# Turning the gated networks' products in 32x32 blocks on VectorE and through memory, in place of TensorE transposes

## The reference, cut to what matters

```python
def _swiglu(xn, w_gate, w_up, w_down):
    return (jax.nn.silu(xn @ w_gate) * (xn @ w_up)) @ w_down

f = _swiglu(_rmsnorm(h, ffn1_pre_g[i]), ffn1_w_gate[i], ffn1_w_up[i], ffn1_w_down[i])
h = h + 0.5 * _rmsnorm(f, ffn1_post_g[i])
# the token mixer stands between the two
f = _swiglu(_rmsnorm(h, ffn2_pre_g[i]), ffn2_w_gate[i], ffn2_w_up[i], ffn2_w_down[i])
h = h + 0.5 * _rmsnorm(f, ffn2_post_g[i])
```

## Time and profile before

| | us |
|---|---|
| median of 3 runs | 1149.78 (1149.68 to 1149.98) |
| the profiled execution's own time | 1149.85 |
| its span, first to last instruction | 1148.1 |
| TensorE busy in it | 1137.0 |
| VectorE busy | 741.5 |
| ScalarE busy | 589.3 |
| GpSimd busy | 106.0 |

### The profile page before, as it was taken

One profiled execution on the slowest core, in us unless ns is written; L12 is line 12 of the kernel. 1 busy time (PEld: TensorE's weight loads), 2 busy tenths in 40 slices (PEclk: granted clock), 3 DMA queues, 4 the chain that ended last, 5 costly groups with the idle time before them and its releaser, 6 DMA issues.

```text
span 1148.1 us, 16462 instructions
## 1 busy us (share of the span) xinstructions
PE 1137.0 (99%) x6408; PEld 993.1 (86%) x6408; DVE 741.5 (65%) x931; ACT 589.3 (51%) x788; POOL 106.0 (9%) x162
## 2 busy tenths in 40 slices
PE   9999999999999999999999999999999999999997
PEld 8998888888889999988888898899888888889885
DVE  6866686657777888754664554665866566545465
ACT  6774654445565766543544443564554364444353
POOL 6410211000011000000000000200500010000020
PEclk9999999999999999999999999999999999999999
DMA  9743653465634765564665556465457477654642
GB/s 258 206 156 92 223 187 111 161 202 185 218 130 141 251 205 175 188 213 148 213 211 182 187 177 207 152 217 179 146 186 238 147 229 235 191 169 175 218 132 72
DMA packets 122894, 209.81 MB, mean 183 GB/s; under 512 B 10965, under 2 KB 58186, under 8 KB 122827
## 3 DMA queue, kind: packets, MB, share of 16 engines
q1 hardware_dynamic: 119225, 198.64, 54.2%
q10 hardware_dynamic: 3506, 10.23, 2.7%
q0 software_dynamic: 96, 0.01, 0.1%
HBM read 207.67 MB, written 1.18 MB: 182 GB/s over the span
## 4 chain that ended last, share of the span: by engine, by line
PE 95%; DVE 3%; DMA 1%; ACT 1%; issue 0%; POOL 0%; POOLq 0%; DVEq 0%; SPq 0%; ACTq 0%
PE ACCP L869 28%; PE ACCP L871 28%; PE ACCP L870 28%; PE SMP L1070 3%; DVE CONVF L2303 1%; DVE LO L2178 1%; PE SMP L1063 1%; DMA RAW<-in_w_in_dram 1%; PE SMP L1023 1%; PE SMP L1017 1%; PE SMP L1018 1%; DMA X<-in_x_dram 0%; PE SMP L1223 0%; PE SMP L1239 0%; PE SMP L1408 0%; PE SMP L1504 0%
## 5 line engine op out<-in xcount | busy, mean ns | idle before, releaser
L2178 DVE TENSOR_TENSOR LO<-RAW,HI 128x1024 fp32r<-128x1024 f32 x365 | 438.1, 1237 | 232.1 <-ACT HI L1609 225.9
L1609 ACT ACTIVATE HI<-RAW 128x1024 fp32r<-128x1024 f32 x366 | 370.4, 1054 | 271.8 <-PE ACCP L871 223.5
L869 PE MATMUL ACCP<-HI,XH 128*128 128x512 f32 x704 | 277.4, 394 | 0.0
L871 PE MATMUL ACCP<-HI,XL 128*128 128x512 f32 x704 | 274.4, 390 | 0.0
L870 PE MATMUL ACCP<-LO,XH 128*128 128x512 f32 x704 | 274.0, 389 | 0.0
L869 PE MATMUL ACCP<-XH,HI 128*128 128x256 f32 x640 | 182.0, 284 | 0.6 <-DVE CONVF L2303 0.6
L871 PE MATMUL ACCP<-XH,LO 128*128 128x256 f32 x640 | 181.1, 283 | 0.0
L870 PE MATMUL ACCP<-XL,HI 128*128 128x256 f32 x640 | 181.1, 283 | 0.0
L871 PEld LDWEIGHTS ACCP<-HI,XL 128*128 128x128 f32 x704 | 132.1, 188 | 27.9
L870 PEld LDWEIGHTS ACCP<-LO,XH 128*128 128x128 f32 x704 | 132.3, 188 | 26.3
L869 PEld LDWEIGHTS ACCP<-HI,XH 128*128 128x128 f32 x704 | 132.2, 188 | 26.2
(11 more groups left out here) (416 smaller groups left out, 1145.0 us busy)
## 6 DMA issues: line engine op xcount, KB each, us to landing
RAW<-in_w_in_dram SPq DMA_DIRECT2D x104, 512.0 KB, 4.5
RAW<-in_w_up_dram SPq DMA_DIRECT2D x44, 512.0 KB, 4.4
RAW<-in_ffn_w_gate_dram SPq DMA_DIRECT2D x44, 512.0 KB, 4.5
RAW<-in_ffn_w_up_dram SPq DMA_DIRECT2D x44, 512.0 KB, 4.4
RAW<-in_ffn_w_down_dram SPq DMA_DIRECT2D x44, 512.0 KB, 4.1
RAW<-in_w_down_dram SPq DMA_DIRECT2D x22, 512.0 KB, 4.3
RAW<-in_w_out_dram SPq DMA_DIRECT2D x8, 512.0 KB, 4.4
RAW<-in_w_mkv_dram SPq DMA_DIRECT2D x8, 512.0 KB, 5.0
```

The lines of the kernel that those rows point to most:

```text
L869: pe.matmul(dst, lhs[0], rhs[0], start=start, stop=False)
L871: return pe.matmul(dst, lhs[1], rhs[0], start=False, stop=stop)
L1609: act.activation(HI[:, n % RING, half_of(half)], RAW[:, n % RAWS, half, :], ACT.Copy).then_inc(hi_ready, 1)
L2178: dve.tensor_tensor(LO[:, s, c], RAW[:, n % RAWS, half, :], HI[:, s, c].bitcast(f32), ALU.subtract).then_inc(lo_ready[s], 1)
```

## The change

TensorE no longer turns the products of chunks. For each chunk and m, DVE transposes UBT in 32x32 blocks into TURNED, SP writes TURNED to a scratch tensor in memory (one transfer of 256 KB) and reads it back into BLOCKS with the blocks on their right partitions (four transfers of 64 KB, each to 32 partitions in pieces of 128 floats). ACT copies BLOCKS to HH and DVE takes the lo part from BLOCKS. The 20 entries of SMALL fall away. The loads of the down weights are issued in the same function as those of gate and up, with the moves between them. The steps on ACT and DVE for chunk c-1 stand at the end of chunk c in place of its start, and those of the last chunk behind the second split of the down phase. The handling of `pT` (a small transposed input of the last stage) on ACT and DVE goes behind the splits of `down2`.

```diff
-def hidden_turns(phase):
-    return [f"{phase}.h{c}{m}" for c in range(GLU_CHUNKS) for m in range(NT)]
-SMALL += open_turns("norm_ffn", "up") + norm_turns("norm_f1") + hidden_turns("ffn1")
+SMALL += open_turns("norm_ffn", "up") + norm_turns("norm_f1")
...
+        TURNED, BLOCKS = at("TURNED", 62, [P, NT, 4, 4, 32]), at("BLOCKS", 66, [P, NT, 4, 4, 32])
+        hidden_rows = nc.dram_tensor("scratch_hidden", (NT, 4, 32, 4, 128), f32)
...
+        def chunks_before(phase, c):
+            return GLUS.index(phase) * GLU_CHUNKS + c
...
+            def hidden_out(phase, c):
+                n = chunks_before(phase, c)
+                for m in range(NT):
+                    sp.wait_ge(turned, NT * n + m + 1)
+                    wait(sp, blocks_in, 64 * NT * n)
+                    sp.dma_start(hidden_rows[m].rearrange("b f r c -> (b f) r c"), TURNED[:, m].rearrange("p r k t -> p r (k t)")).then_inc(turned_out, 16)
+
+            def hidden_in(phase, c):
+                n = chunks_before(phase, c)
+                sp.wait_ge(turned_out, 16 * NT * (n + 1))
+                wait(sp, blocks_split, NT * n)
+                for m in range(NT):
+                    for r in range(4):
+                        sp.dma_start(BLOCKS[32 * r:32 * r + 32, m].rearrange("p b k t -> p b (k t)"),
+                                     hidden_rows[m, :, :, r, :].rearrange("b f c -> f b c")).then_inc(blocks_in, 16)
+
+            def hidden_moves(phase, loaded):
+                for c in range(GLU_CHUNKS):
+                    if loaded == 4 * c + 9:
+                        hidden_out(phase, c)
+                    if loaded == 4 * c + 10:
+                        hidden_in(phase, c)
+
+            def load_glu(phase, gate, up, down):
                 for j in range(GLU_T):
                     q = j // 2
                     load(phase, Turn(j), t_block((gate, up)[q % 2], 512 * (q // 2), j % 2))
+                    hidden_moves(phase, j)
                 for i, m in enumerate((gate, up)):
                     load(phase, Turn(GLU_T + i), f_block(m, 512 * GLU_CHUNKS))
+                    hidden_moves(phase, GLU_T + i)
+                behind = ("down1", "down2")[GLUS.index(phase)]
+                for j in range(COUNT[behind]):
+                    load(behind, Turn(j), d_block(down, j))
+                    hidden_moves(phase, GLU_T + 2 + j)
...
-            def turn_hidden(phase, c):
-                for m in range(NT):
-                    acc_is_taken(pe, phase, Turn(2 * c + 1), m)
-                    turn_four(f"{phase}.h{c}{m}", lambda h: UBT[:, m, h * P:(h + 1) * P])
                 for j in range(T_OPEN[phase], GLU_T):
                     t_half(phase, j, XH, XL)
-                    if j % 4 == 0:
-                        turn_hidden(phase, j // 4 - 1)
                 f_gemm(phase, Turn(GLU_T), XH, XL)
-                turn_hidden(phase, GLU_CHUNKS - 1)
...
-                        for m in range(NT):
-                            small_is_taken(pe, f"{up}.h{k // 4}{m}")
+                        pe.wait_ge(blocks_split, NT * (chunks_before(up, k // 4) + 1))
...
+            def hidden_hi(phase, c):
+                act.wait_ge(blocks_in, 64 * NT * (chunks_before(phase, c) + 1))
+                for m in range(NT):
+                    copy(HH[:, 4 * c:4 * c + 4, tok(m)].rearrange("p k (b t) -> p k b t", b=4), BLOCKS[:, m].rearrange("p b k t -> p k b t"), h_hi)
+
                 for c in range(GLU_CHUNKS):
                     a = Turn(2 * c)
                     split_ahead(phase, Turn(4 * c))
-                    if c:
-                        hidden_hi(c - 1)
...
                     for j in range(1, 4):
                         split_ahead(phase, Turn(4 * c + j))
+                    if c:
+                        hidden_hi(phase, c - 1)
...
+            def hidden_down_splits(phase, down):
+                for j in range(COUNT[down] - RING):
+                    split_ahead(down, Turn(j))
+                    if j == 1:
+                        hidden_hi(phase, GLU_CHUNKS - 1)
...
             glu_steps("ffn2")
+            hidden_down_splits("ffn2", "down2")
             small_is_done(act, "pT")
             copy(PH[:, :, :], by_head(small("pT"), SEQ), p_hi)
-            down_splits("down2")
...
+            def hidden_turn(phase, c):
+                for m in range(NT):
+                    wait(dve, turned_out, 16 * NT * chunks_before(phase, c))
+                    acc_is_taken(dve, phase, Turn(2 * c + 1), m)
+                    dve.transpose(TURNED[:, m].rearrange("p r k t -> p k r t"), UBT[:, m, :].rearrange("p (k r t) -> p k r t", r=4, t=32)).then_inc(turned, 1)
+
+            def hidden_blocks_lo(phase, c):
+                part = slice(4 * c, 4 * c + 4)
+                for m in range(NT):
+                    dve.wait_ge(h_hi, hidden_hi_count(phase, c) + m + 1 + (c == GLU_CHUNKS - 1))
+                    dve.tensor_tensor(HL[:, part, tok(m)].rearrange("p k (b t) -> p k b t", b=4), BLOCKS[:, m].rearrange("p b k t -> p k b t"),
+                                      HH[:, part, tok(m)].rearrange("p k (b t) -> p k b t", b=4).bitcast(f32), ALU.subtract).then_inc(blocks_split, 1)
...
                     split_ahead(phase, Turn(4 * c))
-                    if c:
-                        hidden_lo(c - 1)
...
                     split_ahead(phase, Turn(4 * c + 3))
+                    hidden_turn(phase, c)
+                    if c:
+                        hidden_blocks_lo(phase, c - 1)
                 a, b = Turn(GLU_T), Turn(GLU_T + 1)
                 split_ahead(phase, a)
-                hidden_lo(GLU_CHUNKS - 1)
```

More of the change, by code:

```diff
@@ L153 @@
 SMALL += ["mkT0", "mkT1", "mqT0", "mqT1", "mS0a", "mS0b", "mS1a", "mS1b", "mP0a", "mP0b", "mP1a", "mP1b", "mo0", "mo1"]
-def hidden_turns(phase):
-    return [f"{phase}.h{c}{m}" for c in range(GLU_CHUNKS) for m in range(NT)]
-SMALL += open_turns("norm_ffn", "up") + norm_turns("norm_f1") + hidden_turns("ffn1")
+SMALL += open_turns("norm_ffn", "up") + norm_turns("norm_f1")
 SMALL += norm_turns("norm_mix2") + ["sguw"] + [f"sgu{g}" for g in range(4)] + [f"y2_{c}{m}" for c in range(2) for m in range(NT)]
-SMALL += norm_turns("norm_f2") + hidden_turns("ffn2") + ["pT", "norm_ple.00", "norm_ple.01", "ple.0a", "ple.0b", "ple.1a", "ple.1b", "norm_ple.10", "norm_ple.11"]
+SMALL += norm_turns("norm_f2") + ["pT", "norm_ple.00", "norm_ple.01", "ple.0a", "ple.0b", "ple.1a", "ple.1b", "norm_ple.10", "norm_ple.11"]
 SMALL_ORDER = {name: i for i, name in enumerate(SMALL)}
@@ L405, in build @@
         a_base, a_act, b_base, h_ready, h_hi, h_lo = sems("a_base a_act b_base h_ready h_hi h_lo")
+        turned, turned_out, blocks_in, blocks_split = sems("turned turned_out blocks_in blocks_split")
         post_sq, tap_done, dve_mix = sems("post_sq tap_done dve_mix")
@@ L586, in load_pairs @@
                 repeat(sp, 0, FT // 2, 2, step)
-            def load_glu(phase, gate, up):
+            def hidden_out(phase, c):
[19 more added lines that the diff above has]
+            def load_glu(phase, gate, up, down):
                 for j in range(GLU_T):
@@ L658, in _ @@
             load_down("down", w["w_down"])
-            load_glu("ffn1", w["ffn1_w_gate_2"], w["ffn1_w_up_2"])
-            load_down("down1", w["ffn1_w_down_2"])
+            load_glu("ffn1", w["ffn1_w_gate_2"], w["ffn1_w_up_2"], w["ffn1_w_down_2"])
             load_t("mix_v", w["w_in_2"], DM)
@@ L670, in _ @@
             load_d("mix_o", w["w_o_2"])
-            load_glu("ffn2", w["ffn2_w_gate_2"], w["ffn2_w_up_2"])
-            load_down("down2", w["ffn2_w_down_2"])
+            load_glu("ffn2", w["ffn2_w_gate_2"], w["ffn2_w_up_2"], w["ffn2_w_down_2"])
             load_d("ple_e", w["ple_w_proj_2"])
@@ L2039, in glu_steps @@
                 split_ahead(phase, a)
-                hidden_hi(GLU_CHUNKS - 1)
                 split_ahead(phase, b)
@@ L2043, in glu_steps @@
                 copy(HH[:, 4 * GLU_CHUNKS:FT, :], UBF[:, :, :], h_hi)
+            def hidden_down_splits(phase, down):
[3 more added lines that the diff above has]
+                        hidden_hi(phase, GLU_CHUNKS - 1)
             glu_steps("ffn1")
-            down_splits("down1")
+            hidden_down_splits("ffn1", "down1")
             post_norm_behind("down1", "norm_mix2", "mix_v")
@@ L2686, in _, with hidden_hi_count, hidden_down_splits @@
             norm_behind("down", "norm_f1", "ffn1")
-            def glu_steps(phase):
[L2691 to L2699, removed]
+            def hidden_hi_count(phase, c):
+                return (GLUS.index(phase) + 1) * (FT // 2) + NT * c
+            def hidden_turn(phase, c):
[9 more added lines that the diff above has]
+                                      HH[:, part, tok(m)].rearrange("p k (b t) -> p k b t", b=4).bitcast(f32), ALU.subtract).then_inc(blocks_split, 1)
+            def hidden_down_splits(phase, down):
+                for j in range(COUNT[down] - RING):
+                    split_ahead(down, Turn(j))
```

(5 more changed lines are left out.)

## The result

The changed kernel takes 1140.71 us (median of four runs, 1140.46 to 1141.54), the kernel before 1149.78. The ratio is 0.9923, with a 95% interval of 0.9911 to 0.9935. The prediction said 1140.9, with a range from 1140.3 to 1144.

A forecast was written before the change was run, and what follows sets the result against it. The prediction took TensorE, which never waits in the gated networks, as the bound: 1149.85 us less 8.9 for removed transposes, plus 0 for hidden additions, is 1140.95; it said 1140.9, with a range from 1140.3 to 1144.

The forecast's parts named there:

- What bounds the kernel: Gated networks: TensorE never waits, so an instruction taken from it shortens the kernel by its place in the stream.
- The price of a turn: TensorE's stream: eight transposes take 0.89 us from start to start, 0.87 between networks' blocks; ten turns give 8.9 us.
- VectorE: Each chunk: two added 128x512 transposes of 0.69 us (0.5 to 1.2), 1.4 us together, hidden; next split just reached.
- ScalarE: Copies to HH: 586 ns from PSUM become 633 from SBUF, 1 us in all, hidden; data for BLOCKS should long be there.
- SP and DMA: Each chunk: ten added transfers, 4.2 us of DMA work, share 0.77; SP waits at most 1 us; TensorE unaffected.
- The room: Every block: VectorE's lo part has 12.7 us before TensorE wants it; loads have 2.9 us before ACT waits.
- My last sentence: Sign of being wrong: VectorE transposes above 5 us each would fill a chunk and make VectorE the bound.
- partial giving back at the opening: Opening of each network: DMA share reaches 0.88, loads fall behind, TensorE waits; 1142 to 1147, say 1144; chance 0.07.
- The slower rival: Reads in 512 B pieces overfill the DMA engines from 0.119 us a piece; at 0.15 us, 1161 us; chance 0.05.
- the ruinous gather: Eight reads of a chunk take 19 times a 512 KB load, 86 us; kernel about 1920 us; chance 0.01.

The follow-up runs named there:

- doubling: The kernel before, with every TensorE transpose of UBT done twice into the same place (160 in place of 80): 1158.74 us, ratio 1.0077.
- the run without turns: The kernel before, with HH and HL of the chunks read from UBT unturned, no transposes and nothing in their place: 1141.05 us, ratio 0.9923.
- with 4 times: The changed kernel with each of VectorE's transposes done 4 times, one behind the other: 1140.98 us, ratio 0.9921.
- run with 8 times: The changed kernel with each of VectorE's transposes done 8 times, one behind the other: 1200.7 us, ratio 1.0438.
- spread out: The changed kernel with 118 added VectorE transposes, in chunks 1 to 4 in groups of 3 or 4 between block splits: 1150.26 us, ratio 1.0004.

## Why the prediction was right

- **What bounds the kernel:** right. TensorE without waits in the gated networks was the whole argument, and the list of waits after is the same.
- **The price of a turn, 0.89 us for eight transposes:** right. Predicted 8.9 us; measured 9.1 by removal, 8.7 by doubling. The 272 ns of a record would have given 80 x 0.272 = 21.8 us. Start to start is the price. That the time came within 0.2 us of the forecast is in part luck: the interval of the ratio is over 1 us wide to either side. The Trainium skill's figure of 390 ns for one transpose (VectorE: DVE Perf Modes, The three transpose paths), which is for bf16, doesn't hold as a price in this stream.
- **VectorE:** right in size, 688 ns for 690, and the next split was just reached, as worked out.
- **ScalarE:** 614 ns for 633, hidden, and no wait for BLOCKS.
- **SP and DMA:** the writes took 5.2 us to land; the sum allowed 2.0 to 4.5, so SP's wait was up to 4.5 us, not 1. The share was 0.80 for 0.77. Harmless as predicted. The transfers' whole work can be read from the queue line: 57.2% against 53.8% in the run without turns, 3.4% of 1139 us, or 3.9 us of all 16 engines a chunk, where 4.2 was taken. This share scatters between runs with equal traffic (56.3% with 4 times; 54.2% of a longer span in the kernel before), so the work may be as little as 1.9 us a chunk.
- **The room:** the step that was wrong, though it decided nothing here. I read 12.7 us for each block, plus 2.9 for loads. The run with 8 times shows that the two aren't independent: what holds VectorE holds the loads. A burst of 5.9 us is hidden, one of 11.7 us costs 6 us a chunk. My last sentence has VectorE as the bound above 5 us a transpose. 8 x 0.74 = 5.9 us for each token half is beyond that, but by VectorE's work alone it would cost (23.5 - 21.8) x 10 = 17 us, and it cost 60. Where between 2.9 and 5.9 us the cost begins, no run tells.
- **The rivals:** partial giving back at the opening did not come, though the share there was 0.85, near the 0.88 worked out. The slower rival (0.119 us for a small piece) and the ruinous gather were far off: the strided reads land in 2.3 us, in 2.7 with pieces of 128 B. The Trainium skill's factor of 19 (VectorE: DVE Perf Modes, The three transpose paths) compares a plain strided copy with a transposing DMA, where the innermost destination stride is large. Here the pieces end contiguous and VectorE turns inside the blocks, and no run has a transposing DMA, so these runs don't test that rule.

## What to carry to other kernels

Where the list of waits shows that TensorE never stops in a stretch, price what you take from it by the distance of starts with and without it, and expect that and no more. Work can then be moved to any engine with gaps, but look at how it lies there: in one piece it stops whoever needs that engine to free a buffer, while spread out nearly the same work cost a sixth as much (9.5 us against 60). And count the issue of transfers as work of the engine that issues them: four in place of one on ScalarE, with the one behind them, took it 3.0 us more and brought TensorE a wait of 1.1 us, more than the 0.9 expected from eight transposes.

## What the runs showed of the hardware that I had not expected

- Four times as many read pieces, of 128 B in place of 512 B, added at most 8.6 ns of an engine for each packet, at a DMA share of 0.81 to 0.88 in the chunks of `ffn1`, and nothing to the time.
- 80 more transposes on VectorE, where its burst already decided the time, cost 0.74 us each, their wait on each other's semaphore included; alone an instruction is 0.69.
- A transfer that takes ScalarE 0.52 us to issue took 1.89 in the one trace where it stands behind four others of 64 KB in pieces of 128 B. Why was not tested.
- Behind a burst on the last engine of a ring (load, copy, subtract), that engine itself waits for the reload: 4.0 to 4.5 us of a period on VectorE, both with 4 and with 8 times.
